# Level 0 of a chunked recurrence: row sums of query times key in place of four full products

## The reference

```
q = silu(q_raw);  k = (1 - lb) * sigmoid(-f_raw)
logf = log(lb + (1 - lb) * sigmoid(f_raw));  b = cumsum(logf)
decay = exp(b[t] - b[s]) for s <= t, else 0
A[t, s] = sum over d of q[t, d] * decay[t, s, d] * k[s, d]
out[t]  = sum over s of A[t, s] * v[s]  +  (q[t] * exp(b[t])) @ S
```

## Time and profile before

| | |
|---|---|
| median of 3 runs | 1905.6 us (1905.28 to 1905.85) |
| profiled execution, its own time | 1905.25 us |
| its span, first to last instruction | 1903.0 us |
| granted TensorE clock, mean share | 0.999 |
| PE busy | 1889.7 us (99%) |
| DVE, ACT, POOL busy | 1120.1, 761.0, 188.9 us |

### The profile page before, as it was taken

How to read it: one execution, slowest core, us unless ns; L and a number is a source line. 1 busy time by engine, 2 the same in 40 slices (tenths; PEclk the granted TensorE clock), 3 DMA queues, 4 the chain that set the end, 5 groups by cost and what they waited for, 6 DMA issues and landing times.

```text
span 1903.0 us, 24976 instructions
## 1 busy us (share of the span) xinstructions
PE 1889.7 (99%) x8660; PEld 1537.2 (81%) x8660; DVE 1120.1 (59%) x1595; ACT 761.0 (40%) x1084; POOL 188.9 (10%) x193
## 2 busy tenths in 40 slices
PE   9999999999999999999999999999999999999999
PEld 8888888888888777887788888888888888887887
DVE  7665567777777777777644334434555555556332
ACT  6543333332333373224533443445444544554111
POOL 3500000000000003442000000000111111110000
PEclk9999999999999999999999999999999999999999
DMA  7344244444444426675222222222212222123441
GB/s 278 111 155 177 77 164 158 174 176 171 161 158 172 155 89 221 232 249 190 69 92 84 74 91 91 91 74 84 89 66 79 75 88 88 66 89 123 145 151 66
DMA packets 50406, 244.69 MB, mean 129 GB/s; under 512 B 5688, under 2 KB 6968, under 8 KB 29760
## 3 DMA queue, kind: packets, MB, share of 16 engines
q1 hardware_dynamic: 49920, 241.02, 35.7%
q10 hardware_dynamic: 448, 3.17, 0.4%
HBM read 235.75 MB, written 8.41 MB: 128 GB/s over the span
## 4 chain that ended last, share of the span: by engine, by line
PE 93%; DVE 4%; ACT 2%; issue 1%; DVEq 0%; ACTq 0%; another core or an unknown queue 0%
PE ps_p L561 26%; PE ps_p L563 26%; PE ps_p L562 26%; PE ps_s L679 2%; PE ps_o L697 2%; PE ps_s L859 1%; PE ps_t L687 1%; DVE w_lo L1371 1%; PE ps_x L580 1%; DVE act_lo L1887 0%; ACT act_hi L1165 0%; ACT w_hi L946 0%; PE ps_p L818 0%; PE ps_t L889 0%; PE ps_s L618 0%
## 5 line engine op out<-in xcount | busy, mean ns | idle before, releaser
L561 PE MATMUL ps_p<-act_hi,w_hi 128*128 128x512 f32 x2272 | 924.3, 407 | 4.6 <-DVE act_lo L1750 1.7
L563 PE MATMUL ps_p<-act_hi,w_lo 128*128 128x512 f32 x2272 | 886.7, 390 | 0.0
L562 PE MATMUL ps_p<-act_lo,w_hi 128*128 128x512 f32 x2272 | 886.2, 390 | 0.0
L561 PEld LDWEIGHTS ps_p<-act_hi,w_hi 128*128 128x128 f32 x2272 | 427.2, 188 | 95.1 <-issue 7.2
L563 PEld LDWEIGHTS ps_p<-act_hi,w_lo 128*128 128x128 f32 x2272 | 426.5, 188 | 91.5
L562 PEld LDWEIGHTS ps_p<-act_lo,w_hi 128*128 128x128 f32 x2272 | 427.5, 188 | 87.5 <-issue 5.3
L946 ACT ACTIVATE w_hi<-raw 128x2048 fp32r<-128x2048 f32 x154 | 294.5, 1912 | 424.2 <-PE ps_p L563 405.7
L1371 DVE TENSOR_TENSOR w_lo<-raw,w_hi 128x2048 fp32r<-128x2048 f32 x153 | 350.8, 2293 | 122.9 <-ACT w_hi L946 112.2
L1633 DVE CUSTOM_DVE_ANT_0 mkv<-mkv,c_all 128x1024 f32<-128x1024 f32 x96 | 145.3, 1550 | 1.0 <-DMA mkv<-ada_dram 0.7
L2075 POOL TENSOR_TENSOR hz<-hqk,hd 128x128 f32<-128x128 f32 x56 | 38.5, 688 | 751.7 <-DVEq L1945 700.5
L2062 POOL TENSOR_TENSOR ssq_a<-ssq_a,wk 128x512 f32<-128x512 f32 x15 | 37.8, 2523 | 736.9 <-ACT wk L1185 736.9
(11 more groups left out here) (292 smaller groups left out, 1741.1 us busy)
## 6 DMA issues: line engine op xcount, KB each, us to landing
raw<-wt_dram SPq DMA_DIRECT2D x156, 1024.0 KB, 4.8
mkv<-ada_dram SPq DMA_DIRECT2D x96, 512.0 KB, 4.6
qkv<-xT_dram SPq DMA_DIRECT2D x16, 256.0 KB, 2.8
spill_dram<-Y SPq DMA_DIRECT2D x16, 256.0 KB, 2.5
hqk<-spill_dram SPq DMA_DIRECT2D x16, 256.0 KB, 2.7
out_dram<-wk SPq DMA_DIRECT2D x16, 256.0 KB, 2.0
Y<-xT_dram SPq DMA_DIRECT2D x3, 1024.0 KB, 9.9
mem_raw<-memT_dram SPq DMA_DIRECT2D x4, 512.0 KB, 11.5
```

Of the source, the lines that this page charges most:

```text
L561: mm(o, wh, hi[:, k, 0:n], start=at == 0, stop=False)
L562: mm(o, wh, lo[:, k, 0:n], start=False, stop=False)
L563: last = mm(o, wl, hi[:, k, 0:n], start=False, stop=at == KT - 1)
```

## The change

Level 0 becomes a product on DVE, a rounding on ACT, a subtraction on DVE and two row sums on TensorE. The tiles `sq3_hi` and `sq3_lo` of the output norm are used for it as well, and `wk[:, 2, :]`. Every row of the result holds the same sum, and the mask of `masked(0)` picks the diagonal as before. TensorE's hook moves from behind step 9 to behind step 10 of projection 2. All added lines are in the loop over the eight heads.

```diff
@@ TensorE, level(0) in hg
-                            pe.wait_ge(query_ready.sem, query_ready.at("hg", i, 1))
-                            for t in range(QT):
-                                c = slice(t * P, (t + 1) * P)
-                                last = mm(ps_s[:, 0, c], hk[:, c], hq[:, c], start=True, stop=True,
-                                          skip_group_check=True)
+                            pe.wait_ge(diag_ready.sem, diag_ready.at("hg", i, 1))
+                            mm(ps_s[:, 0, :], ones_r[:, :], sq3_hi[:, :], start=True, stop=False)
+                            last = mm(ps_s[:, 0, :], ones_r[:, :], sq3_lo[:, :], start=False, stop=True)
@@ TensorE, hooks
-                project("hg", i, 2, hooks={9: level(0), 11: level(1), 12: level(2), 15: level(3)})
+                project("hg", i, 2, hooks={10: level(0), 11: level(1), 12: level(2), 15: level(3)})
@@ ACT, hg
                 split("hg", i, 2)
+                act.wait_ge(diag_in.sem, diag_in.at("hg", i, 1))
+                fn(sq3_hi[:, :], wk[:, 2, :], ACT.Copy).then_inc(diag_high.sem, 1)
                 act.wait_ge(side_full.sem, side_full.at("hg", i, 1))
@@ DVE, hg
                 dve.sem_inc(query_ready.sem, 1)
+                o.step(tt(wk[:, 2, :], hq, hk, ALU.mult))
+                o.settle()
+                dve.sem_inc(diag_in.sem, 1)
...
                 diff(3)
+                dve.wait_ge(diag_high.sem, diag_high.at("hg", i, 1))
+                tt(sq3_lo[:, :], wk[:, 2, :], sq3_hi[:, :].bitcast(F32), ALU.subtract).then_inc(diag_ready.sem, 1)
                 masked(0)
```

More of the change, by code:

```diff
@@ L342, in build @@
         decay_exp = Count(sem("decay_exp"), hg=1)
+        diag_in = Count(sem("diag_in"), hg=1)
+        diag_high = Count(sem("diag_high"), hg=1)
+        diag_ready = Count(sem("diag_ready"), hg=1)
         level_diff = Count(sem("level_diff"), hg=NLEV)
@@ L367, in build @@
                 pw_done, squares_ready, squares_added, residual_tile, norm2_tiles, norm2_rows,
-                rms_rows, squares_hi, bias_used, forget_log, decay_ready, decay_exp, level_diff,
+                rms_rows, squares_hi, bias_used, forget_log, decay_ready, decay_exp, diag_in, diag_high, diag_ready, level_diff,
                 level_exps, query_ready, level_in, query_decayed, scores_masked, kv_full, states_ready,
```

## The result

| | before | changed |
|---|---|---|
| median of 18 runs | 1905.63 us (1903.90 to 1906.58) | 1909.70 us (1907.53 to 1910.45) |
| ratio to before, 95% interval | | 1.0021 (1.0014 to 1.0027) |
| profiled execution, its own time | 1905.25 us | 1909.63 us |
| its span | 1903.0 us | 1907.8 us |
| turn of the head loop, mean from the fourth head to the seventh | 52.33 us | 52.83 us |

The change makes the kernel 4.1 us (0.21%) slower. The turn is the sharper number: it grows by 0.50 us, and eight heads of 0.50 us are 4.0 us. Medians of different sets of runs of one kernel differ by a few tenths of a microsecond (1905.28 to 1905.63 for the kernel before). Neighbouring turns in the middle of the loop differ by less than 0.1 us within one trace.

What follows compares the result with a forecast made beforehand. TensorE, busy 1889.7 of 1903.0 us, was taken as the bound, waiting at level 3 on a DVE-POOL chain. 7 x 0.56 + 0.38 = 4.3 us on 1905.25 gives 1909.55, plus 0.35 for the median: 1909.9 us; range 1905.6 to 1912.4.

Steps and rivals of the forecast that it cites:

- TensorE's work: Per head on TensorE: four full products (0.89 us) give way to two row sums (0.47 us), saving 0.42 us.
- Start of the product: DVE's new query-times-key product starts 0.25 us after the query ends, at 1540.69, and takes about 0.69 us.
- POOL held by the product: POOL's first operation waits for DVE's new product, so its second ends at 1542.11 against 1541.63, 0.48 us later.
- Release of the row sums: TensorE begins the row sums at 1544.08, after DVE's subtraction; the wait costs 0.30 of the 0.42 us saved.
- masked(0): On DVE, behind the second row sum: begins at 1544.96 instead of 1544.40, 0.56 us later.
- Level 3: TensorE waits there for POOL's late result and goes on to projection 3 at 1550.06, not 1549.50: 0.56 us per head.
- The last head: The last of eight heads has a little more air before projection 3, so it was taken to lose 0.38 us.
- The sum: Whole kernel: 7 x 0.56 + 0.38 = 4.3 us slower; this case had chance 0.50.
- ACT's copy at nothing: ACT's rounding copy, between the split and `hkn`, moves `hkn` 0.6 us to about 1542.6 and costs nothing.
- Rival A: POOL is unhindered by DVE's new product; the late hook alone delays masked(0): +2.1 us, 1907.7 us, chance 0.22.
- Rival B: POOL's level 3 slips ahead of DVE's split, so the whole saving arrives: -3.4 us, 1902.2 us, chance 0.10.
- Rival C: POOL starts before DVE's new product, with worse interlocking of the two: +5.6 us or more, 1911.2 us, chance 0.18.

Runs made afterwards that it cites:

- the last experiment: Changed kernel with levels 0, 1, 2 behind steps 11, 12, 13, split cut 1280/768 columns, level 3 behind step 0 of projection 3: 1902.03 us.
- the operand experiment: Changed kernel with DVE's new product reading one operand from PSUM instead of SBUF (level 0's values meaningless): 1907.25 us, ratio 1.0009.

## Why the prediction was right

Forecast 1909.9 us, measured 1909.7 us; forecast direction slower, by 0.22%, measured 0.21%. All times below count from the end of step 9.

- **TensorE's work, 0.89 against 0.47 us.** Right. Unhindered, the row sums took 0.46 us in the last experiment (1543.75 to 1544.21). In the changed kernel TensorE reaches step 15, with level 3, 0.15 us earlier than before (5.08 us instead of 5.23), where 0.14 was forecast, and then waits.
- **Start of the product.** Estimated 0.25 us behind the query, measured 0.24. Its duration 0.69, as taken.
- **POOL held by the product.** Estimated 0.48 us later at POOL's second operation; measured 1544.49 + 0.46 = 1544.95, which is -1.11 us against -1.57 before: 0.46. That DVE starts first rested on an estimated lead of 0.07 us, so part of this was luck: it came out (product 1543.52, POOL 1543.60), and no run shows what the other order would have cost. That the meeting is one of SBUF operands is shown by the operand experiment.
- **Release of the row sums.** Estimated 0.88, measured 0.84 (1546.90 - 1546.06). The subtraction took 0.68, not 0.69, and followed closely.
- **masked(0).** Estimated 0.56 late, measured 1.73 - 1.20 = 0.53.
- **Level 3.** Estimated 0.56 late. Projection 3 goes on at 1552.87 - 1546.06 = 6.81, before at 6.30: 0.51. The waits in the rows are 0.84 us, as forecast (0.8).
- **The last head.** Estimated 0.38 us for it, measured 0.46: from step 9's end to the start of projection 3 it takes 1711.35 - 1704.62 = 6.73 us, and took 6.27 before (1706.55 - 1700.28).
- **The sum.** 4.3 us forecast; the seven turns (3.76) and the last head (0.46) give 4.2 by the traces, 4.07 by the medians. The span differs by 4.8 us; 0.57 us of that lies ahead of the end of the first head's step 9 (1334.62 against 1334.05), which the change does not touch.
- **ACT's copy at nothing.** Right: it ran 1544.30 to 1544.93, and DVE needed it at 1546.17.
- **Rival A** was right in its size: with POOL unhindered the forecast was +2.1 us, and the operand experiment gave +1.8 us and a turn of +0.22. But it is not the case that occurs.
- **Rival B** needed POOL to start ahead of DVE's split, and the prediction had it miss by some 0.3 us. It did: POOL was 0.30 us late (1549.62 against 1549.32). Its figure, -3.4 us, is nearly what the last version reached (-3.5 us), but only after the split was cut and hooks were moved; about 0.7 us of that belongs to cutting the split, by the turns, and the full products get that too.
- **Rival C** did not occur, since DVE started first.

## What to carry to other kernels

When one engine is busy 99% of the time, saving work on it pays only if the next hand-over it must wait for does not depend on what the saving delays. Here the profile named it in two rows: a weight load with a short wait for POOL, so without slack, and a POOL operation stretched to 1.64 us by a DVE operation behind the very instruction that the change moved. Look for a long operation that stands in a short-latency chain (the weight split between masked(0) and masked(1)) and cut it to fit the idle time ahead of it before shortening anything else. In this kernel the cut alone gave too little to show in the medians; what it gave was room for the other changes.

## What the runs showed of the hardware

- The wait that the profile puts before a weight load is longer than what it costs. A step with two full products takes 1.04 us without a wait, and 1.07, 1.22 and 1.73 us with waits of 0.18, 0.34 and 0.84 us. So they cost 0.03, 0.18 and 0.69 us, each time some 0.15 less than the wait. Part of the cost falls behind the wait: there the second row sum starts 0.33 us after the first (1546.91 to 1547.24), unhindered 0.23 us (1543.75 to 1543.98).
- Whether a DVE product holds POOL depends on its operands, not on its length: the same POOL operation took 0.93 us beside a product with both inputs in SBUF and 0.47 us beside one with an input in PSUM, and both products took 0.69 us.
- A POOL operation that starts inside a split ended 0.32 us after the split: 2.31 us for it where the split began 0.30 us earlier (changed kernel, 1551.93 against 1551.61), 1.48 us where only half a split was in the way (1548.43 against 1548.11).
- A full float32 product of 128x128 counts 0.22 us on TensorE (0.89 us for four), about as much as a rounded product of 128x512 (0.23 us).
